# Two edits to a one-core encoder-layer kernel: the halves of the sums of y in other slots of the out projection, and x loaded from two queues

## The chip, the cores and the metric

The kernel runs on one core of a Trainium2 chip. The metric is the device time of one execution, in microseconds (us), as the median of several runs. Lower is better.

Names used below: PE is TensorE (the matrix engine), DVE is VectorE, ACT is ScalarE, POOL is GpSimd and SP is SyncE, which does nothing here but issue transfers (DMAs). ACT and POOL can issue transfers too; each of the three has its own queue, and all transfers are carried by the same 16 DMA engines.

## The reference

One layer of a bidirectional hybrid encoder on 512 tokens of width 2048, all in float32:

```
h = rms(x, norm_g)
u = h @ w_in                      # 13312 columns, split into 11 pieces
ya = (hgrn2(hq, hi, hf_fwd, hf_bwd) normed * silu(hgate)) @ w_branch_a
yb = (neighbourhood_attention(nq, nk, nv) * silu(ngate)) @ w_branch_b
y  = sigmoid(m_a) * ya + sigmoid(m_b) * yb
x  = x + y @ w_out
g  = sigmoid(rms(x, ple_norm) @ w_ple_gate)
x  = x + (p @ w_ple) * g
```

What the change touches is the first line (the norm of x, which everything waits for) and the product `y @ w_out`.

## The kernel before

Every float32 product is made from split operands: a factor is written as a rounded part ("hi") and the rest ("lo"), and PE makes hi\*hi, lo\*hi and hi\*lo. ACT writes the hi part of an operand by a copy, DVE the lo part by a subtraction. So each load of weights (512 KB, a tile 128x1024) costs a copy on ACT, a subtraction on DVE and twelve or more matmuls on PE, and the three engines pass it on through rings of three slots (`RING = 3`). Each engine works through its own list of instructions in the order of the code; semaphores (`wait_ge`, `then_inc`) tie the lists together. There is no scheduler: the order is written out by hand.

**The start.** SP issues, in this order, the norm weights (L675), tokens 0 to 127 of x (t = 0, 1 MB), tokens 128 to 255 (t = 1), the first 512 KB of weights (`plain_load(0)`, tile `q_raw`), t = 2, `plain_load(1)`, t = 3, and further weights (L676 to L681). ACT handles each 128 tokens in `token_root(t)`: a square with a running sum over `x_in[:, t]` (L1011) and a root (L1013). It does t = 0 and t = 1 ahead of all else, t = 2 and t = 3 between the copies of the first tile of h (`START_ROOT`). DVE then takes the reciprocal (L1362) and scales the tokens (L1364). PE turns the scaled tokens by 128x128 transposes (`turn_h`, L1984), and starts with the first only when both t = 0 and t = 1 are scaled: `pe.wait_ge(x_normed, 2)`. From there the first product follows, tile by tile.

**The out projection.** `y @ w_out` is made by a seven-product scheme (Strassen-like) of two column groups; `out_group(g)` on PE has 28 steps j = 0 to 27 in each group g. A step is a load of `w_out` (or a sum of two, made by DVE in `o_weight_sum`, L1847) times a block of y or a sum of blocks of y: twelve matmuls. `row_unit(j)` gives the product u and the quarter kp of a step: j 0 to 7 are products 0 and 1 (plain blocks of y), j 8 to 15 products 2 and 3, j 16, 17, 20, 21 product 6, j 18, 19, 22, 23 product 5, j 24 to 27 product 4. Products 2, 3, 6 and 5 take sums of y, numbered 1, 2, 4 and 3. These four sums (128x2048 each) are complete after `y_sums(7)`, at step 2, and have to be split like all operands: ACT writes the hi half in `sy_hl` by `sy_hi(n)` (L1280), DVE the lo half by `sy_lo(n, done)` (L1835), which waits until `done` hi halves are there. PE waits for them at the first step of a product: `SY_AT = {2: 1, 3: 2, 6: 3, 5: 4}` (product: count of lo halves), that is at j = 8, 9, 16 and 18.

In the same steps run: `o_hi` (ACT, L552) and `o_lo` (DVE, L558) for the weights of step j; the last block of y, `y_hi(15)` (ACT, L1258) and `y_lo(15)` (DVE, L1783), needed by PE at step 7; `o_copy` (ACT, L1290); `o_evict` (DVE, L1899), which adds products into the result; and `o_fetch(g, j)` on SP (L828), which brings the weights of later steps once their slot is free: for steps 10 and 11 when `o_lo` of 5 and 7 is done, for 12 to 19 when the weight sum four steps earlier is made, for 20 and 21 when `o_lo` of 18 and 19 is done. POOL brings the old x for the residual (`x2a`, four transfers of 512 KB, L985) as soon as two lo halves are there (`sy_lo_done` 2) and step 4+2t-1 is done on PE.

The lines that tie the halves to their steps, for ACT and for DVE:

```
if g == 0 and j in (3, 4, 6, 8):
    sy_hi({3: 1, 4: 2, 6: 4, 8: 3}[j])
...
if g == 0 and j in (5, 7, 11, 15):
    sy_lo({5: 1, 7: 2, 11: 4, 15: 3}[j], {5: 1, 7: 2, 11: 3, 15: 4}[j])
```

Of the kernel before, what the change touches and what calls it, by code (L numbers as in the profile page):

```python
# [49 lines left out]
def build_kernel(nc, x, p, norm_g, w_in, hgrn_lb, hgrn_onorm, na_qnorm, na_knorm, na_rpb,  # L50
# [5 lines left out]
    NT, KT, PT = S // P, D // P, PLE // P  # L56
# [35 lines left out]
    x_v = x[0].rearrange("(t p) d -> p t d", p=P)  # L92
# [16 lines left out]
    with ExitStack() as ctx:  # L109
        ctx.enter_context(nc.allow_non_contiguous_dma(reason="norm weights, one element per partition"))  # L110

        def sb(name, shape, dt=F32, where=ctx):
            return where.enter_context(nc.sbuf_tensor(name, shape, dt))

        def sem(name):
            return ctx.enter_context(nc.semaphore(name))
# [31 lines left out]
        with ExitStack() as first:  # L148
            x_in = sb("x_in", [P, NT, D], where=first)
# [112 lines left out]
        x_ready = [sem(f"x_ready{t}") for t in range(NT)]  # L262
# [215 lines left out]
        def feature(n):  # L478

            return n // 2 + 8 * (n % 2)  # L480
# [36 lines left out]
        def sy_source(n):  # L517

            if n in (1, 2):
                return sy_raw[:, n - 1]  # L520
            return act_x[:, n - 3, 0:8, S // 2:S]
# [23 lines left out]
        def o_hi(act, g, j):  # L545
            num = U_OUT + OUT_STEPS * g + j
            if j in ROW_SUMS:
                act.wait_ge(o_sum, 16 * g + ROW_SUMS[j])
            else:
                o_wait_raw(act, g, j)  # L550
            act.wait_ge(unit_done, num - 2)
            nc.scalar.activation(w_hi[:, num % RING, :], o_slots[row_slot(j)], ACT.Copy).then_inc(hi_done, 1)  # L552

        def o_lo(dve, g, j):
            num = U_OUT + OUT_STEPS * g + j
            dve.wait_ge(hi_done, num + 1)
            dve.wait_ge(unit_done, num - 2)
            nc.vector.tensor_tensor(w_lo[:, num % RING, :], o_slots[row_slot(j)],  # L558
                                    w_hi[:, num % RING, :].bitcast(F32), ALU.subtract).then_inc(lo_done, 1)
# [85 lines left out]
        def _(sp):  # L645
            def plain_load(i):
                if i >= 6:
                    sp.wait_ge(qlo_done, i - 5)
                g = i // 2
                c = (MA if g % 2 == 0 else MB) + feature(2 + g // 2) * P  # L650
                dst = q_raw[:, i % 6, :].rearrange("p (k n) -> p k n", k=8)
                sp.dma_start(dst, win_v[:, 8 * (i % 2):8 * (i % 2) + 8, c:c + P]).then_inc(p_raw[i % 6], 16)
# [20 lines left out]
                             c_out[:, m % 3]).then_inc(c_stored[m % 3], 16)  # L673

            sp.dma_start(norm_row[:, :], norm_g[0].rearrange("(k p) -> k p", p=P)).then_inc(norm_in, 16)  # L675
            for t in range(NT):  # L676
                sp.dma_start(x_in[:, t, :], x_v[:, t, :]).then_inc(x_ready[t], 16)
                if 1 <= t <= 2:
                    plain_load(t - 1)
            for i in range(2, PLAIN):  # L680
                plain_load(i)  # L681
            for m in range(len(BLOCKS)):
# [316 lines left out]
        def _(act):  # L999
            A = nc.scalar.activation  # L1000


            act.wait_ge(pool_ready, 1)
            A(mean_w[:, :], mean_in[:, :], ACT.Copy).then_inc(mean_ready, 1)
            act.wait_ge(eps_ready, 1)
# [249 lines left out]
            def y_hi(n):  # L1255
                k, tok = feature(n), slice(0, S if n % 2 else S // 2)
                act.wait_ge(y_ready, n + 1)
                A(act_hi[:, k, tok], y_out[n % 2][:, tok], ACT.Copy).then_inc(a_hi_done, 1)  # L1258
# [18 lines left out]
            def sy_hi(n):  # L1277
                act.wait_ge(unit_done, U_OUT)
                act.wait_ge(sy_sum, 32)
                A(sy_hl[:, n - 1, :, 0], sy_source(n), ACT.Copy).then_inc(sy_hi_done, 1)  # L1280

            def o_copy(g):
                act.wait_ge(unit_done, U_OUT + OUT_STEPS * g + 7)
                if g == 0:
                    act.wait_ge(a_lo_done, KT)
                    act.wait_ge(sy_sum, 32)
                else:
                    act.wait_ge(o_ev, ev(g - 1, 9))
                for t in range(2):
                    A(o_u[t], o_bank(0, t), ACT.Copy).then_inc(o_p1, 1)  # L1290

            def token_squares(g, n):
                t, j = n // 2, n % 2
                num = 8 * g + n
                act.wait_ge(o_ev, 22 * g + 22)
                if num:
                    act.wait_ge(x2_sq, num)
                A(pieces(junk[:, :]), x2_block(g, t, j), ACT.Square, accum_out=ssq[:, 2 * g + j, t:t + 1]).then_inc(x2_sq, 1)

            def h2_hi_tile(k):  # L1300
                act.wait_ge(x2_turned, k + 1)
                if k == 0:
                    act.wait_ge(pn_in, 16)
                if k == 8:
                    act.wait_ge(unit_done, U_PLE)
                A(h2_tile(0, k), pieces(h2_bank(k)), ACT.Copy, scale=pn_c[:, k:k + 1]).then_inc(h2_hi, 1)

            for g in range(OUT_GROUPS):
                for j in range(2 if g == 0 else 0, OUT_STEPS):
                    o_hi(act, g, j)  # L1310
                    if g == 0 and j in (3, 4, 6, 8):
                        sy_hi({3: 1, 4: 2, 6: 4, 8: 3}[j])
                    if g == 0 and j == 3:
                        y_hi(KT - 1)
                    if j == 10:
                        o_copy(g)
                    if g == 1 and 8 <= j < 16:
                        token_squares(0, j - 8)
                    if g == 1 and j - 2 in TURN_AT:
                        h2_hi_tile(TURN_AT[j - 2])  # L1320
# [35 lines left out]
        def _(dve):  # L1356
# [407 lines left out]
            def merge_y(n):  # L1764

                slot = n % 2
                if n < 2:
                    dve.wait_ge(gate_ready, 2 * n + 2)
                else:
                    dve.wait_ge(g_in[slot], 16 * (n // 2))  # L1770
                for b in range(2):
                    dve.wait_ge(unit_done, U_BRANCH + branch_unit(n, b) + 1)
                    TT(g_ab[:, slot, b, :], branch_ps(slot, b), g_ab[:, slot, b, :], ALU.mult).then_inc(y_part, 1)
                dve.wait_ge(y_part, 2 * n + 2)
                if n >= 2:
                    dve.wait_ge(a_lo_done, n - 1)
                    dve.wait_ge(sy_sum, 4 * (n // 2))
                TT(y_out[slot], g_ab[:, slot, 0, :], g_ab[:, slot, 1, :], ALU.add).then_inc(y_ready, 1)
# [6 lines left out]
            def y_sums(m):  # L1785

                one, two = slice(0, S // 2), slice(S // 2, S)
                s1, s2, s3, s4 = (sy_source(n)[:, m, :] for n in (1, 2, 3, 4))
                dve.wait_ge(y_ready, 2 * m + 2)
                if m == 0:  # L1790
                    dve.wait_ge(z_lo_done, 2 * H)
                TT(s3, y_out[0][:, one], y_out[0][:, two], ALU.subtract).then_inc(sy_sum, 1)
                dve.wait_ge(sy_sum, 4 * m + 1)
                TT(s2, y_out[1][:, two], s3, ALU.subtract).then_inc(sy_sum, 1)
                dve.wait_ge(sy_sum, 4 * m + 2)
                TT(s1, s2, y_out[0][:, one], ALU.add).then_inc(sy_sum, 1)
                TT(s4, y_out[1][:, one], s2, ALU.subtract).then_inc(sy_sum, 1)
# [35 lines left out]
            def sy_lo(n, done):  # L1833
                dve.wait_ge(sy_hi_done, done)
                TT(sy_hl[:, n - 1, :, 1], sy_source(n), sy_hl[:, n - 1, :, 0].bitcast(F32), ALU.subtract).then_inc(sy_lo_done, 1)  # L1835
# [70 lines left out]
            for g in range(OUT_GROUPS):  # L1906
                for j in range(2 if g == 0 else 0, OUT_STEPS):
                    o_lo(dve, g, j)
                    if g == 0 and j == 2:
                        merge_y(KT - 1)  # L1910
                        y_sums(7)
                    if g == 0 and j in (5, 7, 11, 15):
                        sy_lo({5: 1, 7: 2, 11: 4, 15: 3}[j], {5: 1, 7: 2, 11: 3, 15: 4}[j])
                    if g == 0 and j == 6:
                        y_lo(KT - 1)
                    if j in O_AT[g]:
                        o_evict(g, O_AT[g][j])
                    if g and j in O_AFTER:
                        o_evict(g - 1, O_AFTER[j])
                    if j + 2 in ROW_SUMS:  # L1920
                        o_weight_sum(g, j + 2)
                    if g == 1 and j - 2 in TURN_AT:
                        h2_lo_tile(TURN_AT[j - 2])
# [475 lines left out]
```

## Time and profile before

| | us |
|---|---|
| median of 3 runs | 1796.1 (1795.31 to 1796.79) |
| the profiled execution, its whole time | 1796.85 |
| the profiled execution, span from first to last instruction | 1795.1 |
| PE busy in that span | 1763.7 |
| granted TensorE clock | 1.0 throughout |

The profile is of one execution. Its rows come in several views. The page has the busy time of each engine. The list of waits says who waited for whom. The timeline gives the instructions of an engine in order of time: start, length, engine, line, operation, and in square brackets the idle time before it with what ended it. The list of transfers gives, for a stretch of time, each queue's packets and megabytes with the share of the 16 DMA engines' time, and the time from a transfer's issue to its landing. Queue q1 carries what SP issues, q0 what POOL issues. Matmuls overlap, so the start of the next one is a better measure of a step than the length of one.

### The profile page before, as it was taken

Reading aid. Unit: us, or ns where it says so; the run is one execution under the profiler, and the core shown is the slowest. Engines: PE = TensorE matmul, PEld = TensorE weight load, DVE = VectorE, ACT = ScalarE, POOL = GpSimd, SP = SyncE. Lnnn points to the kernel's source line nnn. Section 1 sums busy time; section 2 is a strip of 40 time slices with the busy share of each in tenths; the row PEclk is TensorE's granted clock in tenths of the full one; section 3 lists DMA queues with packets and bytes.
Section 4 is the critical chain, followed back from the end, with each engine's and each line's share of the span. In section 5 each row is a group of like instructions: output and inputs, shape, how many; then the busy total and the mean of one; then the engine's idle time right before and its main releaser. Section 6 shows DMA issues by size and latency. Waiting matters only on the chain.

```text
span 1795.1 us, 23833 instructions
## 1 busy us (share of the span) xinstructions
PE 1763.7 (98%) x9241; PEld 1513.3 (84%) x9241; DVE 1282.5 (71%) x1546; ACT 865.2 (48%) x1169; POOL 197.8 (11%) x204
## 2 busy tenths in 40 slices
PE   6999999999999999999999999999999999999998
PEld 5899999888888888888888888888888877888887
DVE  6977777777687777878787878794555588874433
ACT  7444444434474747565656575655222343544221
POOL 4000000000040403031313121221000000000000
PEclk9999999999999999999999999999999999999999
DMA  7354444675723333333333333334555456542332
GB/s 225 89 141 122 117 124 144 213 246 176 200 84 109 87 112 87 100 88 106 93 106 92 95 104 94 103 105 144 164 144 150 152 195 230 184 141 94 118 118 82
DMA packets 287269, 236.81 MB, mean 132 GB/s; under 512 B 7977, under 2 KB 232264, under 8 KB 286656
## 3 DMA queue, kind: packets, MB, share of 16 engines
q1 hardware_dynamic: 284064, 225.48, 41.9%
q0 software_dynamic: 3104, 9.96, 1.7%
q8 instruction: 65, 1.06, 0.2%
q14 instruction: 36, 0.29, 0.1%
HBM read 215.00 MB, written 20.41 MB: 131 GB/s over the span
## 4 chain that ended last, share of the span: by engine, by line
PE 90%; DVE 5%; issue 2%; DMA 2%; ACT 1%; SPq 0%; DVEq 0%; ACTq 0%
PE mm_ps L2054 13%; PE mm_ps L2052 13%; PE mm_ps L2053 13%; PE ax_ps L2039 2%; PE ax_ps L2041 2%; PE ax_ps L2040 2%; PE ax_ps L2052 2%; PE ax_ps L2054 2%; PE ax_ps L2053 2%; PE mm_ps L2277 2%; PE mm_ps L2278 2%; PE mm_ps L2276 2%; PE mm_ps L2040 2%; PE mm_ps L2041 2%; PE mm_ps L2039 2%
## 5 line engine op out<-in xcount | busy, mean ns | idle before, releaser
L364 DVE TENSOR_TENSOR w_lo<-w_raw,w_hi 128x1024 fp32r<-128x1024 f32 x188 | 235.9, 1256 | 252.2 <-ACT w_hi L355 252.1
L2052 PE MATMUL mm_ps<-act_hl,w_hi 128*128 128x512 f32 x960 | 383.3, 399 | 0.0
L355 ACT ACTIVATE w_hi<-w_raw 128x1024 fp32r<-128x1024 f32 x188 | 198.4, 1056 | 373.0 <-PE mm_ps L2054 157.7
L2054 PE MATMUL mm_ps<-act_hl,w_lo 128*128 128x512 f32 x960 | 375.2, 391 | 0.0
L2053 PE MATMUL mm_ps<-act_hl,w_hi 128*128 128x512 f32 x960 | 374.8, 390 | 0.0
L2054 PEld LDWEIGHTS mm_ps<-act_hl,w_lo 128*128 128x128 f32 x960 | 180.3, 188 | 38.6
L2053 PEld LDWEIGHTS mm_ps<-act_hl,w_hi 128*128 128x128 f32 x960 | 180.6, 188 | 36.1
L2052 PEld LDWEIGHTS mm_ps<-act_hl,w_hi 128*128 128x128 f32 x960 | 180.6, 188 | 35.7
L1056 ACT ACTIVATE q_hi<-q_raw 128x1024 fp32r<-128x1024 f32 x84 | 87.6, 1057 | 141.7 <-DVE q_raw L1420 81.2
L1411 DVE TENSOR_TENSOR q_lo<-q_raw,q_hi 128x1024 fp32r<-128x1024 f32 x84 | 101.8, 1224 | 52.6 <-ACT q_hi L1056 52.1
L928 POOL TENSOR_TENSOR key<-key,low_h 128x512 f32<-128x512 f32 x16 | 16.8, 1051 | 804.8 <-ACT key L1163 804.8
L453 ACT ACTIVATE q_hi<-r_in 128x1024 fp32r<-128x1024 f32 x56 | 59.5, 1062 | 91.0 <-PE ax_ps L2093 49.4
L1577 DVE TENSOR_TENSOR dif<-cum 128x512 f32<-128x512 f32 x96 | 95.0, 1003 | 0.5
L459 DVE TENSOR_TENSOR q_lo<-r_in,q_hi 128x1024 fp32r<-128x1024 f32 x56 | 68.5, 1223 | 28.3 <-ACT q_hi L453 28.2
L2039 PE MATMUL ax_ps<-s_hl,q_hi 128*128 128x256 f32 x288 | 81.7, 284 | 1.8 <-DVE q_lo L1411 1.8
L2041 PE MATMUL ax_ps<-s_hl,q_lo 128*128 128x256 f32 x288 | 81.6, 283 | 0.0
L2040 PE MATMUL ax_ps<-s_hl,q_hi 128*128 128x256 f32 x288 | 81.6, 283 | 0.0
L1654 DVE RECIPROCAL rms<-rms 128x512 f32<-128x512 f32 x24 | 80.2, 3343 | 0.0
L941 POOL TENSOR_TENSOR lev_k<-lev_k,key 128x256 f32<-128x256 f32 x64 | 70.0, 1103 | 72.2 <-ACT lev_k L1127 72.2
L1420 DVE TENSOR_TENSOR q_raw<-q_raw 128x1024 f32<-128x1024 f32 x48 | 58.4, 1217 | 0.0
L2039 PEld LDWEIGHTS ax_ps<-s_hl,q_hi 128*128 128x128 f32 x288 | 55.4, 192 | 2.2 <-issue 2.2
L2040 PEld LDWEIGHTS ax_ps<-s_hl,q_hi 128*128 128x128 f32 x288 | 55.4, 192 | 0.0
(373 smaller groups left out, 4187.3 us busy)
## 6 DMA issues: line engine op xcount, KB each, us to landing
w_raw<-in_w_in SPq DMA_DIRECT2D x120, 512.0 KB, 3.8
q_raw<-in_w_in SPq DMA_DIRECT2D x56, 512.0 KB, 6.0
r_in<-in_w_in SPq DMA_DIRECT2D x56, 512.0 KB, 4.6
w_raw<-in_w_out SPq DMA_DIRECT2D x36, 512.0 KB, 5.2
w_raw<-in_w_ple_gate SPq DMA_DIRECT2D x32, 512.0 KB, 3.8
w_raw<-in_w_branch_a SPq DMA_DIRECT2D x16, 512.0 KB, 4.0
w_raw<-in_w_branch_b SPq DMA_DIRECT2D x16, 512.0 KB, 4.0
r_mid<-in_w_out SPq DMA_DIRECT2D x16, 512.0 KB, 5.6
```

Source lines behind the costliest of these rows:

```text
L355: nc.scalar.activation(w_hi[:, s, :], w_raw[:, r, :], ACT.Copy).then_inc(hi_done, 1)
L364: nc.vector.tensor_tensor(w_lo[:, s, :], w_raw[:, r, :], w_hi[:, s, :].bitcast(F32), ALU.subtract).then_inc(lo_done, 1)
L1056: A(q_hi[:, p_slot(b, u), :], quarter(b, P_QUARTER[u]), ACT.Copy).then_inc(qhi_done, 1)
L1411: TT(q_lo[:, s, :], quarter(b, P_QUARTER[u]), q_hi[:, s, :].bitcast(F32), ALU.subtract).then_inc(qlo_done, 1)
L1577: TT(dif[:, n % 2, :].rearrange("p (b w) -> p b w", w=w), v, ref, ALU.subtract).then_inc(dif_ready, 1)
L1654: nc.vector.reciprocal(rms[:, :], rms[:, :]).then_inc(rinv_ready, 1)
L2039: MM(bank, wh, m[:, 0], start=k == 0, stop=False)
L2040: MM(bank, wh, m[:, 1], start=False, stop=False)
L2041: mm = MM(bank, wl, m[:, 0], start=False, stop=k == 7)
L2052: MM(bank, wh, m_hi[:, k0 + k, :], start=start and k == 0, stop=False)
L2053: MM(bank, wh, m_lo[:, k0 + k, :], start=False, stop=False)
L2054: mm = MM(bank, wl, m_hi[:, k0 + k, :], start=False, stop=stop and k == kn - 1)
```

## The change

On SP the loop over t now takes t = 0 and t = 2 only, each followed by one load of weights. ACT issues t = 1 and t = 3 as its first two instructions, ahead of its first activation. In the out projection of group 0, DVE writes the lo halves of the sums of y in steps 3, 4, 7 and 10 in place of 5, 7, 11 and 15, in the same order (1, 2, 4, 3). `y_hi(15)` moves from step 3 to step 4 on ACT, and `y_lo(15)` from step 6 to step 5 on DVE. The steps of ACT's hi halves stay.

```diff
@@ SP @@
-            for t in range(NT):
+            for t in (0, 2):
                 sp.dma_start(x_in[:, t, :], x_v[:, t, :]).then_inc(x_ready[t], 16)
-                if 1 <= t <= 2:
-                    plain_load(t - 1)
+                plain_load(t // 2)
             for i in range(2, PLAIN):
                 plain_load(i)
@@ ACT @@
+            for t in (1, 3):
+                act.dma_start(x_in[:, t, :], x_v[:, t, :]).then_inc(x_ready[t], 16)
             act.wait_ge(pool_ready, 1)
@@ ACT, out projection @@
-                    if g == 0 and j == 3:
+                    if g == 0 and j == 4:
                         y_hi(KT - 1)
@@ DVE, out projection @@
-                    if g == 0 and j in (5, 7, 11, 15):
-                        sy_lo({5: 1, 7: 2, 11: 4, 15: 3}[j], {5: 1, 7: 2, 11: 3, 15: 4}[j])
-                    if g == 0 and j == 6:
+                    if g == 0 and j in (3, 4, 7, 10):
+                        sy_lo({3: 1, 4: 2, 7: 4, 10: 3}[j], {3: 1, 4: 2, 7: 3, 10: 4}[j])
+                    if g == 0 and j == 5:
                         y_lo(KT - 1)
```

How the instructions stand. First the beginning of SP's list, before; `q_raw` is the first weights:

```order
L675 DMA norm_row<-in_norm_g 16x128
L677 DMA x_in<-in_x 128x2048 x2
L652 DMA q_raw<-in_w_in 128x8x128
L677 DMA x_in<-in_x 128x2048
L652 DMA q_raw<-in_w_in 128x8x128
L677 DMA x_in<-in_x 128x2048
```

The same place on SP now:

```order
L675 DMA norm_row<-in_norm_g 16x128
L677 DMA x_in<-in_x 128x2048
L652 DMA q_raw<-in_w_in 128x8x128
L677 DMA x_in<-in_x 128x2048
L652 DMA q_raw<-in_w_in 128x8x128 x7
```

Two transfers are gone from SP's list; the first weights come right behind t = 0. They stand at the head of ACT's list, which now begins:

```order
L1003 DMA x_in<-in_x 128x2048 x2
L1005 ACT_TABLE_LOAD
L1005 ACTIVATE mean_w<-mean_in 128x128
L1012 ACTIVATE x_sq,stat<-x_in 128x2048
L1014 ACT_TABLE_LOAD
```

So t = 1 no longer stands behind t = 0 in one queue. The second place is DVE in the out projection, from `o_lo(3)` on, before (L558 is `o_lo`, L1835 `sy_lo`, L1783 `y_lo(15)`, L1847 a weight sum):

```order
L558 TENSOR_TENSOR w_lo<-w_raw,w_hi 128x1024
L558 TENSOR_TENSOR w_lo<-r_gate,w_hi 128x1024
L558 TENSOR_TENSOR w_lo<-w_raw,w_hi 128x1024
L1835 TENSOR_TENSOR sy_hl<-sy_raw,sy_hl 128x8x256
L558 TENSOR_TENSOR w_lo<-r_gate,w_hi 128x1024
L1783 TENSOR_TENSOR act_hl<-m_lev,act_hl 128x512
L1847 TENSOR_TENSOR r_mid<-r_mid 128x1024
L558 TENSOR_TENSOR w_lo<-w_raw,w_hi 128x1024
L1835 TENSOR_TENSOR sy_hl<-sy_raw,sy_hl 128x8x256
L1847 TENSOR_TENSOR r_mid<-w_raw,r_mid 128x1024
L558 TENSOR_TENSOR w_lo<-r_mid,w_hi 128x1024
```

The same place on DVE now (each line number is one higher):

```order
L558 TENSOR_TENSOR w_lo<-w_raw,w_hi 128x1024
L1836 TENSOR_TENSOR sy_hl<-sy_raw,sy_hl 128x8x256
L558 TENSOR_TENSOR w_lo<-r_gate,w_hi 128x1024
L1836 TENSOR_TENSOR sy_hl<-sy_raw,sy_hl 128x8x256
L558 TENSOR_TENSOR w_lo<-w_raw,w_hi 128x1024
L1784 TENSOR_TENSOR act_hl<-m_lev,act_hl 128x512
L558 TENSOR_TENSOR w_lo<-r_gate,w_hi 128x1024
L1848 TENSOR_TENSOR r_mid<-r_mid 128x1024
L558 TENSOR_TENSOR w_lo<-w_raw,w_hi 128x1024
L1836 TENSOR_TENSOR sy_hl<-act_x,sy_hl 128x8x256
L1848 TENSOR_TENSOR r_mid<-w_raw,r_mid 128x1024
```

Ahead of the weights of step 4 stands one half more than before, ahead of those of step 5 two more, ahead of those of steps 6 and 7 one more. The third half stands where the second stood, right ahead of the weight sum of step 9, and the last two have left steps 11 and 15.

## Rows read from the trace of the kernel before

**Rows 1.** The page: busy time of each engine, share of the span, instructions

```profile
PE 1763.7 (98%) x9241; PEld 1513.3 (84%) x9241; DVE 1282.5 (71%) x1546; ACT 865.2 (48%) x1169; POOL 197.8 (11%) x204
```

**Rows 2.** List of waits of PE, out projection: total us, times, longest

```profile
PE ax_ps L2329 <- DVE w_lo L558: 4.2, 6, 1.5
...
PE mm_ps L2329 <- DVE w_lo L558: 2.2, 3, 1.0
```

**Rows 3.** Timeline of the start: start us, length us, instruction, idle before and releaser

```profile
1.26 0.89 SPq L677 DMA_DIRECT2D x_in<-in_x  x2
...
6.26 1.91 ACT L1011 ACTIVATE x_sq<-x_in 128x2048 f32<-128x2048 f32 x1 [3.86 <-DMA x_in<-in_x]
...
9.58 0.29 ACT L1013 ACTIVATE stat<-stat,eps_c 128x1 f32<-128x1 f32 x1
...
11.02 1.91 ACT L1011 ACTIVATE x_sq<-x_in 128x2048 f32<-128x2048 f32 x1 [1.15 <-DMA x_in<-in_x]
...
13.58 1.37 DVE L1364 TENSOR_SCALAR x_in<-x_in,stat 128x2048 f32<-128x2048 f32 x1
...
15.00 2.40 PE L1984 MATMUL ax_ps<-ident,x_in 128*128 128x128 f32 x10 [12.28 <-DVE x_in L1364]
...
17.38 1.90 ACT L1011 ACTIVATE x_sq<-x_in 128x2048 f32<-128x2048 f32 x1
```

**Rows 4.** Packets, MB, share, in 1-4, 4-6.2, 6.2-11 (two rows) and 11-14 us

```profile
q1 hardware_dynamic: 83, 0.43, 47.0%
...
q1 hardware_dynamic: 126, 0.90, 105.2%
...
q1 hardware_dynamic: 469, 0.96, 66.6%
q0 software_dynamic: 185, 0.02, 17.6%
...
q1 hardware_dynamic: 769, 1.05, 112.6%
```

**Rows 5.** Transfers from 1446 to 1452 us; the last row is the page's

```profile
q0 software_dynamic: 296, 1.10, 53.0%
q1 hardware_dynamic: 463, 0.88, 41.6%
...
x2a<-in_x POOLq DMA_DIRECT2D x3, 512.0 KB, 7.8
w_raw<-in_w_out SPq DMA_DIRECT2D x3, 512.0 KB, 9.9
...
w_raw<-in_w_out SPq DMA_DIRECT2D x36, 512.0 KB, 5.2
```

**Rows 6.** Timeline of ACT in the out projection, step 3

```profile
1429.60 1.92 ACT L1280 ACTIVATE sy_hl<-sy_raw 128x2048 fp32r<-128x2048 f32 x1 [2.27 <-DVE act_x L1797]
```

**Rows 7.** Timeline of DVE in the out projection, steps 5, 6, 11 and 20

```profile
1435.76 1.23 DVE L558 TENSOR_TENSOR w_lo<-w_raw,w_hi 128x1024 fp32r<-128x1024 f32 x1 [1.52 <-ACT w_hi L552]
1436.90 2.28 DVE L1835 TENSOR_TENSOR sy_hl<-sy_raw,sy_hl 128x2048 fp32r<-128x2048 f32 x1
1439.11 1.22 DVE L558 TENSOR_TENSOR w_lo<-r_gate,w_hi 128x1024 fp32r<-128x1024 f32 x1
...
1457.23 1.23 DVE L1847 TENSOR_TENSOR r_gate<-w_raw,r_gate 128x1024 f32<-128x1024 f32 x1 [0.54 <-DMA w_raw<-in_w_out]
...
1483.23 1.23 DVE L1847 TENSOR_TENSOR r_mid<-r_mid,w_raw 128x1024 f32<-128x1024 f32 x1 [1.62 <-DMA w_raw<-in_w_out]
```

**Rows 8.** Timeline of PE: first matmul of steps 5, 8, 12 and 21

```profile
1437.15 0.40 PE L2329 MATMUL mm_ps<-w_hi,act_hl 128*128 128x512 f32 x1
...
1447.82 0.47 PE L2329 MATMUL ax_ps<-w_hi,sy_hl 128*128 128x512 f32 x1 [1.53 <-DVE w_lo L558]
...
1459.65 0.50 PE L2329 MATMUL ax_ps<-w_hi,sy_hl 128*128 128x512 f32 x1 [0.66 <-DVE w_lo L558]
...
1485.64 0.50 PE L2329 MATMUL mm_ps<-w_hi,sy_hl 128*128 128x512 f32 x1 [0.93 <-DVE w_lo L558]
```

## The prediction, made before the changed kernel was run

> **What bounds the kernel now.** The page first: PE is busy for 1763.7 us [rows 1] of a span of 1795.1, at the full clock throughout, so no more than 31.4 us can be had without taking work from PE, and the change takes none. The question is which of PE's idle stretches the two edits touch, and what they put in their place. The list of waits and the timeline give two places. At the start PE stands still until 15.00, of which the longest wait is for the scaled second 128 tokens [rows 3]. In the out projection PE waits for lo parts of weights, 4.2 and 2.2 us in nine waits [rows 2]; with the idle instants that this list leaves out and the restarts of the matmul pipeline, step 0 to step 27 of the first group take 81.4 us on PE's timeline where 27 steps of 2.72 us would be 73.4, so 7.9 us are lost there. Everything between the two places is packed on PE: what one of them gains or loses moves the end by the same amount.
>
> **Edit 1: x from two queues.** Before, x is brought in the order in which it is used. t = 0 is issued at 1.26 and ACT begins its square at 6.26, when it lands; t = 1 lands at 11.02, when ACT has been idle for 1.15 us [rows 3]. After the landing of t = 0, ACT needs 9.87 - 6.26 = 3.61 us (square, table load, root) before it can take t = 1, and from the start of that square to PE's first transpose are 15.00 - 11.02 = 3.98 us. So PE starts at the later of (landing of t = 0) + 7.59 and (landing of t = 1) + 3.98. Today the second one decides, 15.00 against 13.85. The most that an earlier t = 1 can give is therefore 1.15 us, and that only if t = 0 still lands at 6.26; as soon as t = 0 lands after 7.41, the edit costs time.
>
> Now t = 1 is issued by ACT at about the same instant as SP's first transfer (0.8, where both lists begin), some 0.45 us ahead of t = 0, which stands behind the norm weights. Both are 1 MB in rows of the same length. Is there room beside t = 0? From 4 to 6.2 us its queue fills the 16 DMA engines (105% share, 0.90 MB in 2.2 us, 410 GB/s) [rows 4]. There is none, so t = 1 takes what it gets from t = 0. What two queues do to each other shows later in the same trace: from 1446 to 1452 POOL's and SP's queues split the engines 53.0% to 41.6%, and SP's 512 KB transfers take 9.9 us to land in place of 5.2 in the median [rows 5]. So I take it that t = 0 and t = 1 now finish nearly together, t = 0 last, when both are moved: 2.1 MB. Lower bound: at 410 GB/s from the first data at 2.5 us or so, 2.5 + 5.1 = 7.6 us. Upper bound: the pace of now, by which t = 1 had landed at 11.0; from 6.2 to 11 the engines were busy for only 66.6 + 17.6 = 84% [rows 4], POOL's small constants among it, and a second queue can fill part of the rest. I take the middle, 9.4 us. PE then starts at 9.4 + 7.6 = 17.0, that is **2.0 us later**, with 7.6 giving 0.2 and 11.0 giving 3.6 us later.
>
> The Trainium skill, "DMA: Bandwidth & Descriptors", section "Issuing engines are not separate DMA queues", says that issuing from several engines saves only the sequencer's time to issue. Rows 5 agree. Taken at its word, the second queue would fill nothing of the 16% and the sum would go by the upper bound, 3.6 us. No number here needs it.
>
> The rest of the edit costs nothing. ACT issues its two transfers while it would wait for t = 0 anyway (3.86 us idle ahead of 6.26 [rows 3]); SP's issue of 0.41 us each is not waited for. The first weights now stand behind t = 0 and beside t = 3, and may land at about 14; ACT wants them at 13.5 and has 1.2 us to spare behind them, plus the 2.0. t = 2 stands behind t = 0 and 512 KB of weights while t = 3 runs in the other queue: with 3.1 + 1.5 MB to move by then, some 17 us; ACT comes to it at 17.38 + 2.0 = 19.4 [rows 3]. t = 3, landing sooner, is not waited for before either. The delay is carried on: from 15 to 89 us the chain that ended last runs through ACT and DVE at work, with no transfer in it that could take it up.
>
> **Edit 2: the lo halves sooner.** A weight operation (o_lo, or a weight sum) takes 1.14 us of DVE from start to start, a half 2.2 (1435.76, 1436.90, 1439.11) [rows 7]. I follow the order by hand, in the times of the trace before; "w(j)" is the weight sum of step j.
> - Step 3: the first hi half begins at 1429.60 and ends at 1431.52 [rows 6]. DVE, in front of it since 1430.6, waits, makes the lo half, and comes to o_lo(4) at 1433.75; before 1433.0. PE's step 4 starts at 1435.0, 0.7 late.
> - Step 4: the second half stands ahead of o_lo(5), which now runs from 1437.1 to 1438.3. PE's step 5 starts at 1438.35 where it started at 1437.15 [rows 8]: **1.2 us late**, the cost of the edit. The moved y_hi and y_lo (0.6 us, 0.7 us) stay behind weights that nobody waits for; y_lo(15) is done by 1439, PE wants it in step 7.
> - Steps 6 and 7: o_lo(6) at 1438.8 (before 1439.1), o_lo(7) at 1441.1. PE steps on without a wait: 1441.2, 1443.9.
> - Step 8: the half at step 7 (1442.2 to 1444.4), w(9), o_lo(8) done at 1446.8. PE's step 8 starts at 1446.85; before 1447.82 [rows 8]. **1.0 us early.**
> - Steps 9 to 11: o_lo(9) at 1447.9, o_lo(10) at 1450.1, the last half at 1451.3, w(12), o_lo(11) done at 1455.8. PE waits 0.8 us for it and starts step 11 at 1455.9, 0.2 early.
> - Step 12: before, w(13) waited until 1457.2 for its weights [rows 7], a transfer issued at 1446.6 that took 10.6 us because POOL's x2a loads began at 1445.7, when the second half was done. Now that half is done at 1437, two of the four x2a loads are through by 1448, and SP issues the weights of step 13 at 1445.6. They land by 1452 or so; w(13) runs at 1455.7 and PE starts step 12 at 1458.7, before 1459.65 [rows 8]: **1.0 us early**.
> - Steps 16 to 21: o_lo(18) used to come behind the half of step 15; now the fetch of step 20 goes out some 1.2 us sooner against PE, while those of 21 to 23 hang on PE's step 16 as before, and w(22) on their landing (1483.23) [rows 7]. With 512 KB less in the queue ahead (1.3 us at 400 GB/s) I credit 0.9 of these. From w(22) on DVE has no idle time until step 26, so the shift stays.
>
> Sum: 1.1 (what step 16 gains, 1.0 and a restart of the matmul pipeline less) + 0.9 = **2.0 us early**. Bounds: 1.1 if the landing of w(22) keeps its distance to step 16, 2.4 if all of the 1.3 comes through. Beneath: nothing, if the weights of step 13 are late again.
>
> **Sum.** +2.0 - 2.0 = 0. The profiled span of 1795.1 stays 1795.1, its time of 1796.85 too, and the median, 0.75 below that, stays **1796.1 us**.
>
> **The rivals.**
> 1. *t = 0 isn't held up* (t = 0 is served first, t = 1 moves up). For it: t = 0 is the first big thing in its queue. Against it: full engines in rows 4, the split in rows 5. PE then starts 1.15 us sooner: -1.15 - 2.0 = -3.15, 1792.95.
> 2. *Slower: t = 0 ends up behind t = 1 and t = 3.* ACT's two transfers are issued back to back (the first two on SP took 0.89 us [rows 3]), so both may stand before t = 0. 3.15 MB have then to go first: 11.0, plus 0.86 MB at 350 GB/s (1.05 MB in 3 us, rows 4) = 2.5, so 13.5, and PE starts at 21.1, 6.1 late. With edit 2: +4.1, 1800.2. It decides for slower once t = 0 lands after 13.0. Against it: equal shares in rows 5.
> 3. *Edit 2 brings nothing*: the early x2a loads meet the weights of steps 10 to 13 in place of 13 to 15, and step 12 is again tied to a landing. Then +2.0, 1798.1. For it: SP's weights suffered most in rows 5. Against it: two loads are spaced by PE's steps now, where three came in 1.6 us.
> 4. *Edit 2 brings more*: without the collision the waits of steps 20 to 26 go too. They are all but 1.2 of the 7.9 us at best: -6.7 + 2.0 = -4.7, 1791.4. Against it: from step 21 DVE has no idle time, and no work is taken from it there.
>
> **How the numbers follow.** Forecast 0.53, rival 1 0.14, rival 2 0.10, rival 3 0.14, rival 4 0.09. 0.2%, or 3.6 us, is about what a measurement of this kernel can tell from no change. Forecast, rival 3 and most of rival 1 lie within it. Faster by more: rival 4 and 0.03 of rival 1, 0.12. Slower by more: rival 2 and 0.01 of rival 3 with the upper bound of edit 1, 0.11. Same: 0.77. The range leaves out the ends of rivals 2 and 4: 1792.6 to 1799.4, which holds -3.15 and +3.6 less a small gain.
>
> **What would show it.** On ACT's timeline the first square begins at 9.4 (7.6 to 11) and the second right behind the root, with no idle time, and PE's first transpose is at 17.0. A square still at 6.3 is rival 1, one after 12.5 rival 2. In the out projection, with times counted from PE's step 0: step 5 1.2 us later, step 8 1.0 earlier, step 12 1.0 earlier, step 21 2.0 earlier; x2a issued some 8 us earlier; no 10 us landing for the weights of step 13. Wrong would be: a start of PE before 15, or step 12 no earlier.

## The result and the profile after

The changed kernel takes 1800.86 us in the median of 10 runs (1799.67 to 1802.7), the kernel before 1796.08 us in 10 runs (1795.31 to 1797.06): 1.0026 times as long, with a 95% interval of 1.0018 to 1.0034. That is 4.8 us slower, a small loss but one clear of the noise, and above the end of the forecast range (1799.4). The profiled execution has a span of 1798.9 us and a whole time of 1800.97; against the 1795.1 of before the span is 3.8 us longer.

The start, on the timeline of all engines of the kernel after (to be held against [rows 3]):

```profile
0.81 0.90 ACTq L1003 DMA_DIRECT2D x_in<-in_x  x2
...
1.26 0.41 SPq L677 DMA_DIRECT2D x_in<-in_x  x1
...
13.80 1.91 ACT L1012 ACTIVATE x_sq<-x_in 128x2048 f32<-128x2048 f32 x1 [10.46 <-DMA x_in<-in_x]
...
17.31 1.89 ACT L1012 ACTIVATE x_sq<-x_in 128x2048 f32<-128x2048 f32 x1
...
19.86 1.29 DVE L1365 TENSOR_SCALAR x_in<-x_in,stat 128x2048 f32<-128x2048 f32 x1
```

A landing is read here, as in the prediction, from the start of the square that waits for it. t = 0 lands at 13.8 us in place of 6.26. The second square follows right behind the first root, so t = 1 was there before ACT asked for it. PE's first transpose follows at 21.20, 6.2 us later than before.

The shares of the queues in the kernel after, in the stretches of [rows 4]: 1 to 4 us, 4 to 6.2 us, 6.2 to 11 us, two rows each (columns: packets, MB, share of the 16 engines). q10 is the queue of what ACT issues:

```profile
q10 hardware_dynamic: 74, 0.61, 60.5%
q1 hardware_dynamic: 32, 0.01, 1.8%
...
q10 hardware_dynamic: 89, 0.60, 67.0%
q1 hardware_dynamic: 34, 0.28, 33.5%
...
q10 hardware_dynamic: 88, 0.72, 35.8%
q1 hardware_dynamic: 82, 0.67, 35.6%
```

Until 4 us SP's queue moves next to nothing: 0.01 MB against 0.61. Those 32 packets are the norm weights (ACT's queue has the same 32 packets in e7 below, where it carries the norm weights alone). So no packet of t = 0 has begun. It is the same up to 4.8 us, when ACT's queue has moved 0.96 MB of its first 1.05 (q10 and q1 of the kernel after, 1 to 4.8 us):

```profile
q10 hardware_dynamic: 117, 0.96, 69.9%
q1 hardware_dynamic: 32, 0.01, 1.4%
```

By 6.2 us ACT's queue has moved 1.21 MB, which is all of t = 1 and the beginning of t = 3, and SP's has 0.28 MB of t = 0. From then on t = 3 and t = 0 share evenly.

The out projection, on PE's timeline of the kernel after: the first matmuls of step 0, then of steps 5, 8, 12 and 21, as in [rows 8]:

```profile
1429.87 0.39 PE L2330 MATMUL mm_ps<-w_hi,act_hl 128*128 128x512 f32 x1
...
1444.95 0.50 PE L2330 MATMUL mm_ps<-w_hi,act_hl 128*128 128x512 f32 x1 [0.32 <-DVE w_lo L558]
...
1453.52 0.47 PE L2330 MATMUL ax_ps<-w_hi,sy_hl 128*128 128x512 f32 x1
...
1465.30 0.39 PE L2330 MATMUL ax_ps<-w_hi,sy_hl 128*128 128x512 f32 x1
...
1489.78 0.40 PE L2330 MATMUL mm_ps<-w_hi,sy_hl 128*128 128x512 f32 x1
```

Step 0 of the kernel before:

```profile
1423.28 0.39 PE L2329 MATMUL mm_ps<-w_hi,act_hl 128*128 128x512 f32 x1
```

So step 0 starts at 1423.28 before and at 1429.87 now, 6.6 us later. Of these 6.2 are the first transpose, and 0.3 are a wait of PE for a lo part (1.36 us, ended at 88.48; before 1.06, ended at 82.03). Counted from step 0, step 5 starts 1.21 us later than before, step 8 0.89 earlier, step 12 0.94 earlier, step 21 2.45 earlier, and by step 27 it is 2.6. From there the distance stays within 0.2. So 6.6 lost at the start and 2.8 won back in the out projection give the 3.8 of the span. The list of PE's waits says the same in two kinds of rows (columns: total us, times, longest). For the start one row of before and one of after:

```profile
PE ax_ps L1984 <- DVE x_in L1364: 13.5, 2, 12.3
...
PE ax_ps L1985 <- DVE x_in L1365: 18.9, 2, 17.9
```

For the out projection the rows of after (before in [rows 2]):

```profile
PE ax_ps L2330 <- DVE w_lo L558: 2.4, 5, 0.6
...
PE mm_ps L2330 <- DVE w_lo L558: 1.9, 3, 0.8
```

The waits for lo parts of `w_out` fell from 6.4 to 4.3 us.

The medians are 4.8 us apart, the profiled executions 4.1 in their whole time (1800.97 and 1796.85) and 3.8 in their span. Most of the difference to the medians is that the profiled execution of before took 0.8 us more than its median and that of after 0.1 more than its own.

### The profile page after: what moved, and what is told of

Read it like the earlier page. It is cut to its first block, busy times and chain, and to the rows that moved or that the text cites. A ratio compares the mean times of both kernels' runs of the same rounds, so it can differ in the third digit from the quotient of the medians.

```text
span 1798.9 us, 23833 instructions
## 1 busy us (share of the span) xinstructions
PE 1764.0 (98%) x9241; PEld 1513.6 (84%) x9241; DVE 1282.5 (71%) x1546; ACT 865.2 (48%) x1169; POOL 198.8 (11%) x204
## 3 DMA queue, kind: packets, MB, share of 16 engines
q8 instruction: 65, 1.06, 0.3%
## 4 chain that ended last, share of the span: by engine, by line
PE 92%; DVE 3%; issue 2%; DMA 1%; ACT 1%; SPq 0%; DVEq 0%; ACTq 0%
PE mm_ps L2055 13%; PE mm_ps L2053 13%; PE mm_ps L2054 13%; PE ax_ps L2040 2%; PE ax_ps L2041 2%; PE ax_ps L2042 2%; PE ax_ps L2053 2%; PE ax_ps L2054 2%; PE ax_ps L2055 2%; PE mm_ps L2277 2%; PE mm_ps L2278 2%; PE mm_ps L2279 2%; PE mm_ps L2040 2%; PE mm_ps L2042 2%; PE mm_ps L2041 2%
```

## The experiments

Twelve kernels were run in three groups, each beside runs of the kernel before on the same chip. These took 1796.84 us (first group), 1796.79 (second) and 1796.68 (third). Positions on a timeline are those of one profiled execution of each kernel. "Distance to step 0" is the start of a step on PE minus that of step 0, compared with the same distance in the trace of before.

**Which edit does what.** The change was taken apart. The first kernel has the queues alone, the second the halves alone.

```diff
# e1_queues_only: the kernel after, with
-                    if g == 0 and j in (3, 4, 7, 10):
+                    if g == 0 and j in (5, 7, 11, 15):
#   and y_hi, y_lo of the last block in their old steps
# e2_halves_only: the kernel before, with
-                    if g == 0 and j in (5, 7, 11, 15):
+                    if g == 0 and j in (3, 4, 7, 10):
#   and y_hi, y_lo of the last block in their new steps
```

> The kernel before with the first edit alone (t = 1 and t = 3 of x from ACT's queue; the lo halves of the sums of y in their old steps). My theory: the whole loss is the late landing of t = 0 (13.8 us in the trace after) and everything behind it is carried on, so PE's first transpose is again near 21.2 and the time is that of after plus the 2.65 us that the second edit gave, about 1803.5. Rival: the two edits hang together and part of the loss arises in the out projection; then this lies under 1802.

Measured: 1802.69 us against 1796.84, ratio 1.0036 (1.0022 to 1.0049), 5.9 us slower. The first square begins at 13.75, PE's first transpose at 21.15. The time is 0.8 us under the expected 1803.5 and not under the rival's 1802. The loss is at the start, and the second edit has no part in it.

> The kernel before with the second edit alone (lo halves in steps 3, 4, 7, 10). My theory: PE's first transpose at 15.0 as before, the steps of the out projection at the same distances from step 0 as after (step 5 1.2 us late, step 8 0.9 early, step 21 2.45 early), and 2.65 us less than before: 1793.4. Rival: part of that gain is there only because the start was late; then it is 1794.5 or more.

Measured: 1794.29 us, ratio 0.9986 (0.9977 to 0.9995), 2.55 us faster than the kernel before on this chip. PE starts at 15.42. The distances to step 0 are those of the kernel after: 1.21 later at step 5, 0.89 earlier at step 8, 0.93 at step 12, 2.44 at step 21. The second edit is a gain of its own, whether the start is late or not. 2.65 us was expected here, and the prediction's sum had 2.0. The expected 1793.4 us was missed by 0.9 because the kernel before, too, took 0.8 us more on this chip than in the first ten runs.

**Why t = 0 came so late.** Four kernels, all with the second edit, vary what stands beside and ahead of t = 0. First, t = 3 goes back to SP, so that ACT issues t = 1 alone:

```diff
# e3_t1_on_act: the kernel after, with
-            for t in (1, 3):
-                act.dma_start(x_in[:, t, :], ...)
+            act.dma_start(x_in[:, 1, :], ...)
#   and on SP, behind plain_load(1):
+            sp.dma_start(x_in[:, 3, :], ...)
```

> The kernel after, but ACT issues t = 1 alone; t = 3 is issued by SP again, behind t = 2 and the second load of weights. My theory: t = 0 was late because t = 3 stood right behind t = 1 in ACT's queue, so that 3.1 MB went before its end; with t = 1 alone it lands at 9.4 to 10.5, PE starts at 17.0 to 18.1 and the time is 1795.5 to 1796.7. Rival: t = 1 beside t = 0, and the small weights rows that now follow t = 0 directly, do it all; then t = 0 lands at 13 or later again and the time is about 1800.5.

Measured: 1797.95 us, ratio 1.0007 (0.9997 to 1.0016), which can't be told from the kernel before. On the timeline of ACT in this kernel t = 0 lands at 10.57:

```profile
10.57 1.91 ACT L1012 ACTIVATE x_sq<-x_in 128x2048 f32<-128x2048 f32 x1 [7.71 <-DMA x_in<-in_x]
```

PE starts at 18.12. So t = 3 behind t = 1 is worth 13.8 - 10.6 = 3.2 us of the landing. The median is 1.1 us over the kernel before on its chip, where 0.6 under to 0.6 over was expected: PE started at the late end of the expected stretch, and the out projection won only 2.26 us by step 21.

> The kernel after with the tokens of the two queues exchanged: ACT issues t = 0 and t = 2, SP t = 1 and t = 3 with the weights between. If what stands first in ACT's queue is served first (it is issued 0.45 us sooner and has no norm weights before it), t = 0 lands at 5.7 and t = 1 at about 13.5: PE starts at 13.5 + 4.0 = 17.5, and the time is about 1796. Rival: SP's or ACT's queue makes no difference and both land when 2.1 MB are moved, 9 to 10 us: t = 0 at 9.5, PE at 17.1, time about 1795.6 (told apart by the landing of t = 0).

```diff
# e4_swap: the kernel after, with the tokens exchanged
#   ACT: t = 0, t = 2;  SP: norm weights, t = 1, plain_load(0), t = 3, plain_load(1)
```

Measured: 1797.45 us, ratio 1.0004 (0.9995 to 1.0013). The timeline of ACT:

```profile
5.84 1.91 ACT L1013 ACTIVATE x_sq<-x_in 128x2048 f32<-128x2048 f32 x1 [2.50 <-DMA x_in<-in_x]
...
13.25 1.91 ACT L1013 ACTIVATE x_sq<-x_in 128x2048 f32<-128x2048 f32 x1 [3.80 <-DMA x_in<-in_x]
```

The tokens have changed places and the landings have too: what is first in ACT's queue lands at 5.8, what is first of the tokens in SP's queue at 13.3. PE starts at 17.15, as 13.25 + 3.9 says. The median is 1.4 us over the expected 1796; the profiled execution, 1796.19, was the fastest of the ten.

Is it ACT's queue that is preferred, or the issue that is sooner? In the fifth kernel the norm weights stand behind t = 0, so that t = 0 and t = 1 are issued at the same instant. In the sixth ACT issues t = 1 behind its first activation, at 1.84 us, after SP's t = 0.

```diff
# e5_norm_behind: e3_t1_on_act, with SP's list
-  norm weights, t = 0, plain_load(0), ...
+  t = 0, norm weights, plain_load(0), ...
# e6_t1_later: e3_t1_on_act, with ACT's list
-  DMA t = 1, mean_w
+  mean_w, DMA t = 1
```

> e3 (ACT issues t = 1 alone), with SP's norm weights moved from ahead of t = 0 to right behind it, so that t = 0 and t = 1 are issued at the same instant, 0.81. Theory A: ACT's queue was ahead of t = 0 because of its 0.45 us and the norm weights before it; then the two share from the start and t = 0 lands at 9.5 or sooner in place of 10.57, PE starts at 17.1 or sooner. Theory B: the engines serve ACT's queue ahead of SP's for another reason; then t = 0 lands at 10.2 or later.

Measured: 1796.51 us, ratio 0.9999 (0.9990 to 1.0009). t = 0 lands at 9.60, PE starts at 17.00. The queues from 1 to 4 and from 4 to 6.2 us in this kernel:

```profile
q1 hardware_dynamic: 34, 0.28, 45.0%
q10 hardware_dynamic: 27, 0.22, 25.0%
...
q1 hardware_dynamic: 53, 0.43, 51.4%
q10 hardware_dynamic: 53, 0.43, 48.3%
```

Issued together, they come to share evenly: 0.71 and 0.65 MB by 6.2 us. No preference for ACT's queue is left, and theory B, which had the landing at 10.2 or later, is out; theory A said 9.5 or sooner. This is the case that the prediction had worked out (9.4 and 17.0), and it isn't the case of the changed kernel.

> e3 with ACT's issue of t = 1 moved behind its first activation (from 0.81 to about 2.4), so that t = 0 has the head start. If the order of issue decides who is served first, t = 0 lands at 6.5 to 8 (not 10.57), t = 1 at 10.5 to 11.5, PE starts at 14.5 to 15.6, and the time is that of the second edit alone (2.55 us under before) within 0.6. If ACT's queue wins whenever it has work, t = 0 lands at 9 or later and PE starts after 16.5.

Measured: 1795.15 us, ratio 0.9993 (0.9983 to 1.0002), 1.6 us under before, where 2.55 within 0.6 was expected. t = 0 lands at 6.61 as the order of issue would have it; t = 1 lands at 12.18 and PE starts at 16.08, 0.7 and 0.5 us beyond the expected ranges. The same two stretches in this kernel:

```profile
q1 hardware_dynamic: 82, 0.42, 50.0%
...
q1 hardware_dynamic: 317, 0.75, 93.9%
q10 hardware_dynamic: 5, 0.04, 4.4%
```

With t = 0 issued 0.58 us ahead (1.26 against 1.84), ACT's queue moves next to nothing until t = 0 is through. And that although SP's queue has the norm weights ahead of t = 0. The order of issue decides, and a lead of 0.58 us is enough to get nearly everything at first. It also shows that the second queue brings t = 1 no sooner: 12.18 here, 11.02 in the kernel before, where it stood behind t = 0.

The tenth kernel asks how the landing turns into time. It is the kernel after, but ACT and DVE take t = 1 before t = 0.

```diff
# e10_roots_swapped: the kernel after, with
-            def token_root(t):
+            def token_root(n):
+                t = (1, 0, 2, 3)[n]
#   and the same in normalise_x
```

> The kernel after, with ACT and DVE taking t = 1 (which lands at 5.7) before t = 0 (13.8). If the late t = 0 costs what it does because the square, table load and root of the other tokens come behind it on ACT, PE starts at 13.8 + 4.0 = 17.8 in place of 21.2 and the time falls by 3.4 us, to 0.9 to 1.5 us over before. Rival: the table load or something else in the chain hangs on other things; then PE starts at 19 or later.

Measured: 1797.49 us against 1796.68, ratio 1.0005 (0.9995 to 1.0014). The timeline of this kernel, ACT and then PE:

```profile
5.90 1.91 ACT L1013 ACTIVATE x_sq<-x_in 128x2048 f32<-128x2048 f32 x1 [2.56 <-DMA x_in<-in_x]
...
13.54 1.91 ACT L1013 ACTIVATE x_sq<-x_in 128x2048 f32<-128x2048 f32 x1 [4.04 <-DMA x_in<-in_x]
...
17.45 2.40 PE L1987 MATMUL ax_ps<-ident,x_in 128*128 128x128 f32 x10 [14.28 <-DVE x_in L1367]
```

PE starts at 17.45 in place of 21.20, 3.75 us sooner. Of these 0.26 come from a landing of t = 0 at 13.54 in place of 13.80. The other 3.5 of the 6.2 us are ACT's square, table load and root of one block of tokens. They lie between the landings when ACT asks first for what lands first, and behind both when it asks for the other.

**What the start can give.** The seventh kernel leaves x in SP's queue and gives ACT the norm weights; the ninth also holds POOL's loads of constants until t = 1 has landed. Both have the second edit.

```diff
# e7_norm_on_act: e2_halves_only, with
-            sp.dma_start(norm_row[:, :], ...)
+            act.dma_start(norm_row[:, :], ...)     # ahead of act.wait_ge(pool_ready, 1)
# e9_pool_later: e7_norm_on_act, with
+            pool.wait_ge(x_ready[1], 16)
             pool.dma_start(cols[:, 0:1], ...)
```

> The second edit alone, x in SP's queue as before, but the norm weights (8 KB) are issued by ACT, so that t = 0 goes out at 0.81 and not 1.26. I expect all landings of x 0.45 us sooner (t = 0 at 5.8, t = 1 at 10.6 to 11.0), PE's start at 14.6 to 15.0, and 0.45 us less than the second edit alone: 3.0 us under before. Rival: t = 1 is held by what the engines do from 6 to 11 us (small constants of POOL), and nothing is gained.

Measured: 1793.69 us, ratio 0.9981 (0.9972 to 0.9990), 3.1 us faster than before. t = 0 lands at 5.86, t = 1 at 10.43, PE starts at 14.34.

> e7 (second edit, norm weights from ACT), with all of POOL's loads of constants waiting until t = 1 of x has landed. If POOL's small packets are what slows t = 1 (they held 10.4% of the engines from 6.2 to 11 us in e7), t = 1 lands at 9.6 to 10.0 in place of 10.43, PE starts at 13.6 to 13.9 in place of 14.34, and the time is 0.5 to 0.7 under e7: 3.7 us under before. Rival: they only fill gaps; t = 1 lands at 10.4 again and the time is e7's.

Measured: 1792.87 us, ratio 0.9979 (0.9970 to 0.9988), 3.8 us faster than before. The timeline of this kernel, ACT and then PE, and the queues from 6.2 to 11 us:

```profile
5.83 1.91 ACT L1012 ACTIVATE x_sq<-x_in 128x2048 f32<-128x2048 f32 x1 [2.97 <-DMA x_in<-in_x]
...
9.34 1.89 ACT L1012 ACTIVATE x_sq<-x_in 128x2048 f32<-128x2048 f32 x1
...
13.23 2.40 PE L1985 MATMUL ax_ps<-ident,x_in 128*128 128x128 f32 x10 [8.93 <-DVE x_in L1365]
```
```profile
q1 hardware_dynamic: 1216, 1.84, 106.0%
```

The same stretch in e7, which differs in POOL's wait alone:

```profile
q1 hardware_dynamic: 864, 1.04, 80.8%
q0 software_dynamic: 180, 0.02, 10.4%
```

With POOL's small packets away, SP's queue alone moves 1.84 MB in the 4.8 us in which it moved 1.04 in e7 and 0.96 before [rows 4], at 106% share. So the idle part of the engines that a second queue was to fill came with POOL's transfers, not from a lack of queues. By what means so few bytes hold up so many, no run here shows. t = 1 is there when ACT comes for it at 9.34, so ACT's own work is now what PE waits for. This is the fastest kernel of the study, but its interval overlaps that of e7: the sooner start is shown, a gain in time over e7 isn't.

**The out projection.** The prediction named two reasons for the gain: the x2a loads move away from the weights of step 13, and `o_lo(18)` no longer stands behind the half of step 15. The eighth kernel was to put x2a back, the eleventh puts back the last half, the twelfth moves x2a away in the old order.

```diff
# e8_x2a_held: e2_halves_only, with
-                pool.wait_ge(unit_done, U_OUT + 4 + 2 * t)
+                pool.wait_ge(unit_done, U_OUT + (8, 8, 8, 10)[t])
# e11_last_half_at_15: e2_halves_only, with
-                    if g == 0 and j in (3, 4, 7, 10):
+                    if g == 0 and j in (3, 4, 7, 15):
# e12_before_x2a_later: the kernel before, with
-                pool.wait_ge(unit_done, U_OUT + 4 + 2 * t)
+                pool.wait_ge(unit_done, U_OUT + (10, 10, 11, 12)[t])
```

> The second edit alone, but POOL's first three x2a loads wait for step 7 on PE, as they came to do before, and so are issued together again. If the gain from step 12 on came from their moving away from the weights of step 13, w(13) waits for a 10 us landing again, step 12 starts at its old distance to step 0 (-0.9 becomes -0.2 to +0.3), and of the 2.55 us about 1 stays. Rival: the gain came from DVE's freer list; then step 12 stays 0.9 early and the time is that of the second edit alone.

Measured: 1794.26 us, ratio 0.9988 (0.9979 to 0.9998), the same as e2. Step 12 is 0.94 early as in e2. But the kernel did not make the collision at step 13 again, as the timelines of SP and POOL show, and behind them the list of transfers (last column: us from issue to landing):

```profile
1445.48 0.37 SPq L828 DMA_DIRECT2D w_raw<-in_w_out  x1
...
1447.22 1.61 POOL L985 DMA_DIRECT2D x2a<-in_x  x3 [191.12 <-PE ax_ps L2331]
```
```profile
w_raw<-in_w_out SPq DMA_DIRECT2D x1, 512.0 KB, 3.8
```

The same issues in the kernel before:

```profile
1446.56 4.91 SPq L828 DMA_DIRECT2D w_raw<-in_w_out  x3
...
1445.70 1.61 POOL L985 DMA_DIRECT2D x2a<-in_x  x3 [189.50 <-DVE sy_hl L1835]
```

In e8 the weights of step 13 go out at 1445.48, 1.7 us ahead of x2a, and land in 3.8 us. In the kernel before they went out at 1446.56, 0.9 us behind the first x2a, and took 10.6. It is the order of issue again, but two things turned it. Counted from step 0, the new place of w(9) in DVE's list made SP's issue 0.9 us sooner (22.4 against 23.3), and the wait for step 7 held x2a until 24.1, where it had gone out at 22.4. The run therefore doesn't tell the two theories apart for step 12 as it was meant to. It did make a collision one step on: the weights of steps 14 and 15 took 8.3 and 9.9 us to land, and no step of PE was later for it (2.45 early at step 21, as in e2).

> The kernel before, with nothing changed but that POOL's x2a loads go out behind steps 9, 9, 10 and 11 on PE, so that none runs beside the weights of step 13. If that collision cost something in the kernel before, it is the 0.5 us that w(13) waited for its weights: these land by 1452 to 1454 in place of 1457.2, and step 12 is 0.5 us earlier against step 0. Rival (after the run with the loads held): the landing decided nothing, and step 12 comes at the same distance within 0.1.

Measured: 1796.75 us, ratio 0.9999 (0.9990 to 1.0009): nothing gained. The weights of step 13 land in 3.7 us in place of 10.6, and step 12 is 0.65 us early against step 0 (it starts at 1458.70, step 0 at 1422.98). By step 21 this is given back, as PE's timeline shows:

```profile
1458.70 0.50 PE L2329 MATMUL ax_ps<-w_hi,sy_hl 128*128 128x512 f32 x1
...
1485.23 0.50 PE L2329 MATMUL mm_ps<-w_hi,sy_hl 128*128 128x512 f32 x1 [1.31 <-DVE w_lo L558]
```

Step 21 is only 0.11 early, after a wait of 1.31 us for its weights. So the collision of transfers, which stood in the chain of before with 10.6 us, was worth 0.6 us at step 12 and nothing at the end. It was also a close thing: in e1, with DVE's old order and x2a issued 0.9 us ahead as before, these weights took 10.0 us in place of 10.6, and step 12 was 0.65 early all the same.

> The second edit alone, with only the last lo half (sum 3) back in step 15. If the gain of steps 16 to 21 came from o_lo(18) no longer standing behind that half, step 21 is no more than about 1.3 to 1.8 us early against step 0 (2.45 with the half in step 10), though steps 11 and 12 are earlier than with it (step 12 1.1 to 1.9 early in place of 0.93). Time 0.3 to 1.0 over the second edit alone. Rival: step 21 hangs on transfers only; then it is 2.4 early again.

Measured: 1793.44 us, ratio 0.9983 (0.9974 to 0.9992), 3.2 us under before. 0.3 to 1.0 over the second edit alone was expected; it is no slower than that (2.55 under before), and the intervals overlap. Step 12 is 1.71 early, in place of 0.93, and step 21 2.91 early, in place of 2.44. The theory had step 21 at 1.3 to 1.8, the rival at 2.4, so the rival is the nearer: the half of step 15 did not hold up the fetch of step 20. The gain between steps 16 and 21 is still 0.3 us smaller than in e2 (1.07 against 1.38). SP's timeline (the fetch of step 20 is `r_mid`):

```profile
1471.38 0.37 SPq L828 DMA_DIRECT2D r_mid<-in_w_out  x1
1474.10 7.79 SPq L828 DMA_DIRECT2D w_raw<-in_w_out  x4
```

The fetch of step 20 (`r_mid`) goes out 0.1 us ahead of PE's step 17 (1471.5), as in the kernel after (1478.79 and 1478.90), and not 1.0 behind it as before (1474.37 and 1473.38). That holds with the half in step 15 or in step 10. In step 10 the half makes PE's step 11 0.6 us later (0.24 early against 0.88).

## Why the prediction was wrong

**The frame held.** PE's start is the later of t = 0 + 7.6 and t = 1 + 4.0: 13.80 and 21.20 are 7.4 apart, 13.54 and 17.45 in e10 3.9 apart. The delay was carried to the end. The cost of a late t = 0 was right, and so was the expectation of a loss at the start. What decided was the landing of t = 0.

**The step that failed** is "t = 0 and t = 1 now finish nearly together, t = 0 last, when both are moved: 2.1 MB", from which the prediction took 9.4 us. It holds when both are issued at once and t = 3 isn't there: 9.60 in e5. The changed kernel differs in two ways. The lead of 0.45 us, which the text named and gave no price, and the norm weights within it, together cost 10.57 - 9.60 = 1.0 us (e3 against e5). t = 3 right behind t = 1, which the text put down as a rival, cost 13.8 - 10.57 = 3.2 us (the kernel after against e3). While t = 0 was still waiting, ACT's queue had all of t = 1 behind it and went on with t = 3. Rival 2 had this mechanism and its price (13.5 for the landing, 21.1 for PE's start, 1800.2 in all, against 13.8, 21.2 and 1800.86), though it put t = 0 behind t = 3 and the two in fact ran side by side. It was given a chance of 0.10. What stood against it in the text was the even split of two queues from 1446 to 1452 [rows 5]. But there both queues had work all the time, and an even split between two queues is what makes t = 0 late: whatever stands in the other queue goes out beside it, t = 3 included. The row spoke for rival 2, not against it.

**The upper bound was no bound.** 11.0 us, "the pace of now", was the pace for 2.1 MB. The queues held 3.1 MB of x ahead of the end of t = 0.

**The idle 16% of the engines** from 6.2 to 11 us was to be filled in part by a second queue. It was not: in the kernel after the three queues together held 72.6% of the engines in this stretch. e9 shows what it came with: without POOL's constants one queue fills them. And t = 1 landed no sooner through a second queue where t = 0 kept its place (12.18 in e6 against 11.02). The Trainium skill, "DMA: Bandwidth & Descriptors", section "Issuing engines are not separate DMA queues", says that only the time to issue is saved; these two landings agree. The prediction's sum by that statement, 3.6 us, fell short of the 6.2 all the same, since it went by the upper bound. In e5 the two queues held 51.4% and 48.3% of the engines from 4 to 6.2 us. The Trainium skill, same page, section "Queues, rings and completion order", says that each DMA engine goes round between the queues for which it has work; that split agrees.

**The second edit** came out as worked out step by step: 1.21 late at step 5 (said 1.2), 0.89 early at step 8 (1.0), 0.25 at step 11 (0.2), 0.94 at step 12 (1.0), 2.45 at step 21 (2.0), and 2.55 us in time in e2. For step 12 the prediction had SP's issue at 1445.6 and a landing by 1452 in the times of before. In the kernel after the issue is 0.9 us sooner against step 0 and takes 5.7 us to land in place of 10.6. Which of its two causes did it, x2a going out sooner or the weights going out sooner, the runs leave open, since either alone is enough: 3.7 us with x2a away (e12), 3.8 with the weights ahead of x2a (e8). In the old order of DVE's list the end of this wait is worth 0.65 us at step 12 (e12); what it is worth in the new order was not tried. For step 21 the earlier fetch of step 20 was right (1.1 us; said 1.2), but its reason, the half of step 15, was not (e11). The gain from step 16 to 21 was put at 0.9. It was 1.38 in the kernel after and 1.07 in e11; in e3, e5 and e10, with the same lists, it was 1.2, 0.4 and 0.4. It follows the landing of the weights of step 22: issued 52 us behind step 0 in all four, they took 5.2 us in the kernel after, 5.6 in e3 and 6.4 in e5 and e10. Why they differ is open. The profiled executions of e5 and e10 also took longer than their kernels' medians, by 2.3 and 0.9 us, so part of it may be the execution and not the kernel. So the 2.45 at step 21 is what these executions showed and not a fixed worth of the edit.

**The forecast of sums.** +6.2 at PE's start and -2.8 in the out projection, with 0.4 us between the two, in place of +2.0 and -2.0.

## What to carry to other kernels

A transfer put in a second queue does not only run beside the first one of the other queue: everything behind it in its own queue runs beside it too. In this kernel that made the transfer that is waited for first land 3.2 us later. What must run beside such a transfer is better issued after it: 0.58 us were enough here (e6). Before a second queue is tried for bandwidth, look at what share of the DMA engines the first one holds; where it is low, look for small transfers from a third queue (here POOL's constants) and hold these back.

When the waited-for work is a chain on one engine, the order of landings matters as much as the last landing: two landings near 6 and 13.5 us cost PE's start 3.5 us more when the engine asks for the late one first (the kernel after against e10).

## What the runs showed of the hardware

- The lead of issue. Two transfers of 1 MB issued at the same instant by SP and ACT had 0.28 and 0.22 MB moved at 4 us (e5). With ACT's 0.45 us ahead, and the norm weights ahead of SP's, it was 0.55 MB against 0.01 (e3). With SP's 0.58 us ahead ACT's had 0.04 MB at 6.2 us, shortly before the first landed at 6.61 (e6). So the one that came second does not get a smaller share from the start: it has nothing at all until the first has moved nearly its whole 1 MB (0.96 MB at 4.8 us in the kernel after), and from then on the two queues share evenly (35.8% and 35.6% from 6.2 to 11 us in that kernel).
- Small packets. 180 packets of POOL with 0.02 MB, from 6.2 to 11 us, went with 1.04 MB for SP's queue (e7); without them it moved 1.84 MB in the same 4.8 us (e9), and t = 1 was there when ACT asked for it at 9.34 and not at 10.43.
